# The start of gate/up, the first loads of down, and the stores of the output, reordered in a one-core decoder step

## The reference, cut to what matters

```python
xn = rmsnorm(x, norm1_g)
h = x + concat([gla(xn), shortconv(xn), chunkmlp(xn)]) @ w_out     # w_out 2048 x 2048
hn = rmsnorm(h, norm2_g)
y = h + (silu(hn @ w_gate) * (hn @ w_up)) @ w_down                 # DFF = 5632
out = rmsnorm(y, final_g)
```

## Time and profile before

| what | value |
|---|---|
| median of 3 runs | 2264.31 us (2262.87 to 2264.34) |
| the profiled execution, its own time | 2265.7 us |
| its span, first to last instruction | 2264.0 us |
| PE busy | 2225.8 us (98%) |
| DVE busy | 1599.5 us (71%) |
| ACT busy | 944.4 us (42%) |
| DMA, mean over the span | 144 GB/s |
| mean granted clock of PE | 0.990 |

### The profile page before, as it was taken

The page is one execution under the profiler, slowest core; times in us unless marked ns, Lnnn a source line. Parts: engine busy times, 40 slices in busy tenths (PEclk is TensorE's granted clock), DMA queues, the critical chain, the costliest instruction groups (busy, mean ns, idle before and its releaser), DMA issues.

```text
span 2264.0 us, 41288 instructions
## 1 busy us (share of the span) xinstructions
PE 2225.8 (98%) x17551; PEld 2214.6 (98%) x17551; DVE 1599.5 (71%) x1866; ACT 944.4 (42%) x1235; POOL 10.5 (0%) x16
## 2 busy tenths in 40 slices
PE   9999999999999989999999999999999899999997
PEld 9999999999999989999999999999999899999997
DVE  6346544447444468888888888888888788887787
ACT  6334122114233344444444444444444444444454
POOL 0000000000000000000000000000000000000000
PEclk9999999999999989999999999999999999999998
DMA  5222242453233223544544544544546865555523
GB/s 192 84 75 76 81 159 91 135 180 119 91 103 113 94 95 103 163 137 137 162 137 137 162 137 136 162 137 138 160 137 204 311 225 200 205 188 187 203 87 108
DMA packets 122693, 325.41 MB, mean 144 GB/s; under 512 B 10603, under 2 KB 55211, under 8 KB 121548
## 3 DMA queue, kind: packets, MB, share of 16 engines
q1 hardware_dynamic: 122044, 323.69, 42.5%
q10 hardware_dynamic: 528, 0.07, 0.0%
HBM read 267.09 MB, written 56.63 MB: 143 GB/s over the span
## 4 chain that ended last, share of the span: by engine, by line
PE 89%; DVE 5%; DMA 2%; issue 1%; ACT 1%; SPq 0%; DVEq 0%; ACTq 0%
PE acc L1073 32%; PE acc L867 31%; PE g L1073 23%; DMA w_raw<-w_d 2%; DVE w_lo L1582 1%; DVE w_s L1603 1%; ACT w_hi L762 1%; DVE trunk L1646 1%; DMA h_dram<-hst 0%; PE g L894 0%; DVE w_raw L1603 0%; PE g L1007 0%; PE g L993 0%; DVE trunk L1774 0%; PE g L999 0%
## 5 line engine op out<-in xcount | busy, mean ns | idle before, releaser
L867 PE MATMUL acc<-op_hi,w_hi 128*128 128x272 f32 x1920 | 402.1, 291 | 1.3 <-DVE w_lo L1191 1.3
L867 PE MATMUL acc<-op_hi,w_lo 128*128 128x272 f32 x1920 | 398.7, 289 | 0.0
L867 PE MATMUL acc<-op_lo,w_hi 128*128 128x272 f32 x1920 | 397.0, 288 | 0.0
L762 ACT CAST w_hi<-w_s 128x1024 fp32r<-128x1024 f32 (+1 forms) x204 | 209.6, 1028 | 366.5 <-DVE w_s L1603 366.5
L1073 PE MATMUL g<-op_hi,w_hi 128*128 128x272 f32 x1056 | 308.1, 292 | 10.8 <-ACT g L738 5.5
L1073 PE MATMUL acc<-op_hi,w_hi 128*128 128x272 f32 x1056 | 306.5, 290 | 5.0 <-DVE w_lo L1582 4.2
L867 PEld LDWEIGHTS acc<-op_hi,w_hi 128*128 128x128 f32 x1920 | 303.7, 189 | 4.5 <-issue 3.5
L1073 PE MATMUL g<-op_hi,w_lo 128*128 128x272 f32 x1056 | 307.3, 291 | 0.0
L1073 PE MATMUL acc<-sg_hi,w_hi 128*128 128x272 f32 x1056 | 306.8, 291 | 0.0
L1073 PE MATMUL acc<-sg_hi,w_lo 128*128 128x272 f32 x1056 | 306.6, 290 | 0.0
L1073 PE MATMUL g<-op_lo,w_hi 128*128 128x272 f32 x1056 | 305.8, 290 | 0.0
(11 more groups left out here) (258 smaller groups left out, 4178.1 us busy)
## 6 DMA issues: line engine op xcount, KB each, us to landing
w_raw<-w_in SPq DMA_DIRECT2D x88, 512.0 KB, 3.3
w_raw<-w_gu SPq DMA_DIRECT2D x88, 512.0 KB, 3.6
w<-w_gu SPq DMA_DIRECT2D x88, 512.0 KB, 3.2
hf_dram<-hf_hi SPq DMA_DIRECT2D x22, 952.0 KB, 6.4
hf_dram<-hf_lo SPq DMA_DIRECT2D x22, 952.0 KB, 8.7
w_raw<-w_out SPq DMA_DIRECT2D x32, 512.0 KB, 3.2
w_raw<-w_d SPq DMA_DIRECT2D x32, 512.0 KB, 4.1
w<-w_d SPq DMA_DIRECT2D x32, 512.0 KB, 3.2
```

Of the source, the lines that this page charges most:

```text
L762: nc.scalar.copy(w_hi[:, (C_ST + n) % RING, 0:w], src[:, 0:w]).then_inc(hi_ready, 1)
L867: last = nc.tensor.matmul(acc[t % 2][:, a, 0:TH], w, x[:, k, a * TH:(a + 1) * TH], start=start and n == 0, stop=stop and n == 2)
```

## The change

Three places are edited.

1. **The first difference forms.** Difference forms 0 and 1 (which now hold combinations 0 and 3, through `T_OF`) are built in two parts: pairs 0 to 6 (1904 columns) during the last tile of w_out, once its first chunk has read tiles 0 to 7, and pair 7 (272 columns) at the end. `forms(i - 1)` moves from the third to the second of a tile pair's four steps. Forms 2 and 3 are built whole, with the weights' lo parts 4 and 5 between them on DVE. PE waits for the last pair only ahead of that pair.
2. **Loads of down.** The loads that SP issued behind the four weight blocks of a unit are now issued between them, by `between(s, j)` after each `load_block(s, j)`. The last spill is split over two units.
3. **The end.** Stores go out from two queues: SP stores tiles 0, 4 and 8 (pairs of tiles), ACT tiles 2, 6, 10 and tiles 12 to 15 as one transfer. The column sums of the last squares move behind the first `factor`.

```diff
+T_OF = (0, 3, 1, 2)
...
+            def between(s, j):
+
+                c, b = divmod(s - FT, BATCHES)
+                if c:
+                    if b and c < NCH - 1 and j != 1:
+                        p = 3 * (b - 1) + (3, 0, 2).index(j)
+                        if p < NP:
+                            sp.wait_ge(chunk_done, done(NP * (FT + BATCHES * c) - NP + p))
+                            load_form(c + 1, p)
+                elif b == 1:
+                    if j == 1:
+                        load_h(1)
+                    elif j == 2:
+                        spill_last(0)
+                    else:
+                        load_form(1, (3, 0).index(j))
+                elif b == 2:
+                    if j == 1:
+                        spill_last(1)
+                    elif j == 2:
+                        sp.wait_ge(hf_out, 32 * (FT // 2))
+                        load_h(2)
+                    else:
+                        load_form(1, 2 + (3, 0).index(j))
+                else:
+                    if j == 1:
+                        load_h(3)
+                    else:
+                        load_form(1, 4 + (3, 0, 2).index(j))
...
                 for j in (1, 3, 0, 2):
                     load_block(s, j)
-                c, b = divmod(s - FT, BATCHES)
-                if c == 0 and b == 1:
-                    load_h(1)
-                    spill_hidden(FT // 2 - 1)
...
+                    between(s, j)
...
-                nc.scalar.copy(opf_hi[:, f], xg[:, :, f, :]).then_inc(t_hi, 1)
+                act.wait_ge(t_made, 3 * end)
+                nc.scalar.copy(opf_hi[:, f, at:end], xg[:, at:end, T_OF[f], :]).then_inc(t_hi, 1)
...
+                if c == C_ST - 2:
+                    form_t_hi(0, 0, HK - 1)
+                    form_t_hi(1, 0, HK - 1)
             single_hi(HK - 1)
-            form_t_hi(0, 0)
-            form_t_hi(3, 1)
+            form_t_hi(0, HK - 1, HK)
+            form_t_hi(1, HK - 1, HK)
             block_hi(0, 4)
-            form_t_hi(2, 2)
-            form_t_hi(1, 3)
+            form_t_hi(2, 0, HK)
             block_hi(0, 5)
+            form_t_hi(3, 0, HK)
             block_hi(0, 6)
...
-                if s == 2 and i:
+                if s == 1 and i:
                     forms(i - 1)
+                if c == C_ST - 2:
+                    form_t_lo(0, 0, HK - 1, 1)
             dve.wait_ge(acc_free, N_IN + KT)
             dve.nop().then_inc(c_read, 8)
+            form_t_lo(1, 0, HK - 1, 2)
             forms(HK - 1)
-            for n, f in enumerate((0, 3, 2, 1)):
-                form_t_lo(f, n)
+            form_t_lo(0, HK - 1, HK, 3)
+            form_t_lo(1, HK - 1, HK, 4)
+            block_lo(0, 4)
+            form_t_lo(2, 0, HK, 5)
+            block_lo(0, 5)
+            form_t_lo(3, 0, HK, 6)
             add_square(KT - 1)
-            for idx in (4, 5, 6):
-                block_lo(0, idx)
+            block_lo(0, 6)
...
+            for a in (1, 0):
+                for k in range(2, NV_OUT, 4):
+                    act.wait_ge(out_v, k // 2 + 1 + (1 - a) * NV_OUT // 2)
+                    act.dma_start(yT[:, k:k + 2, a * TH:(a + 1) * TH], trunk[:, k:k + 2, a * TH:(a + 1) * TH])\
+                        .then_inc(stored, 16)
+                act.wait_ge(out_p, 2 * (2 - a))
+                act.dma_start(yT[:, NV_OUT:, a * TH:(a + 1) * TH], trunk[:, NV_OUT:, a * TH:(a + 1) * TH])\
+                    .then_inc(stored, 16)
...
-            column_sums(0, (rstd[:, 0:TH], sq4[3][:, 0, :], sq4[3][:, 1, :]))
+            column_sums(0, (rstd[:, 0:TH],), True, False)
             pe.wait_ge(diagonals, 1)
             factor(1, pb, 0)
+            pe.wait_ge(part_sq, 4)
+            column_sums(0, (sq4[3][:, 0, :], sq4[3][:, 1, :]), False, True)
             factor(1, pb, 1)
```

More of the change, by code:

```diff
@@ L222, in build @@
         sq4 = [b.rearrange("p (q t) -> p q t", q=2) for b in (tmp[:, 0, :], tmp[:, 1, :], gate, up)]
-        form_hi = (sg_hi[:, 0], opf_hi[:, 0], opf_hi[:, 3], sg_hi[:, 1], opf_hi[:, 1], sg_hi[:, 2], opf_hi[:, 2])
-        form_lo = (sg_lo[:, 0], opf_lo[:, 0], opf_lo[:, 3], sg_lo[:, 1], opf_lo[:, 1], sg_lo[:, 2], opf_lo[:, 2])
+        form_hi = (sg_hi[:, 0], opf_hi[:, 0], opf_hi[:, 1], sg_hi[:, 1], opf_hi[:, 2], sg_hi[:, 2], opf_hi[:, 3])
+        form_lo = (sg_lo[:, 0], opf_lo[:, 0], opf_lo[:, 1], sg_lo[:, 1], opf_lo[:, 2], sg_lo[:, 2], opf_lo[:, 3])
         h_dram = nc.dram_tensor("h_dram", (P, KT, T), F32).ap()
@@ L478, in _, with spill_last @@
             load_h(0)
+            def spill_last(i):
+                d, t = ((hf_dram[0], hf_hi), (hf_dram[1], hf_lo))[i]
+                sp.wait_ge(hf_rdy, FT // 2)
+                sp.dma_start(d.rearrange("f p j t -> p f j t")[:, :, FT // 2 - 1, :], t[:].bitcast(F32))\
+                    .then_inc(hf_out, 16)
+            def between(s, j):
[26 more added lines that the diff above has]
+                        load_form(1, 4 + (3, 0, 2).index(j))
             for s in range(FT + 1, NS):
@@ L481, in _ @@
                     load_block(s, j)
-                c, b = divmod(s - FT, BATCHES)
-                if c == 0 and b == 1:
-                    load_h(1)
-                    spill_hidden(FT // 2 - 1)
[L486 to L494, removed]
+                    between(s, j)
             for a in (1, 0):
-                for k in range(0, KT, 2):
-                    made, n = (out_v, k // 2 + 1) if k < NV_OUT else (out_p, (k - NV_OUT) // 2 + 1)
-                    sp.wait_ge(made, n + (1 - a) * (NV_OUT if k < NV_OUT else KT - NV_OUT) // 2)
+                for k in range(0, NV_OUT, 4):
+                    sp.wait_ge(out_v, k // 2 + 1 + (1 - a) * NV_OUT // 2)
                     sp.dma_start(yT[:, k:k + 2, a * TH:(a + 1) * TH], trunk[:, k:k + 2, a * TH:(a + 1) * TH])\
                         .then_inc(stored, 16)
-            sp.wait_ge(stored, 16 * (1 + 1 + KT))
+            sp.wait_ge(stored, 16 * (1 + 1 + NV_OUT + 2))
             sp.wait_ge(cmv_out, 16)
@@ L716, in single_hi, with form_t_hi @@
                 nc.scalar.copy(sg_hi[:, 1:3, i, :], xg[:, i, 2:4, :]).then_inc(sg_h, 1)
-            def form_t_hi(f, n):
-                if n == 0:
+            def form_t_hi(f, at, end):
+                if end < HK:
+                    act.wait_ge(chunk_done, C_ST - 1)
+                else:
                     act.wait_ge(chunk_done, C_ST)
-                    act.wait_ge(t_made, 3 * HK)
-                nc.scalar.copy(opf_hi[:, f], xg[:, :, f, :]).then_inc(t_hi, 1)
+                act.wait_ge(t_made, 3 * end)
+                nc.scalar.copy(opf_hi[:, f, at:end], xg[:, at:end, T_OF[f], :]).then_inc(t_hi, 1)
             def sides(s):
@@ L1101, in quad, with ready @@
                     if first and idx in T_AT:
-                        pe.wait_ge(t_rdy, T_AT.index(idx) + 1)
+                        f = T_AT.index(idx)
+                        pe.wait_ge(t_rdy, f + 1 if f < 2 else f + 3)
+                        if f < 2:
+                            def ready(j, f=f):
+                                if j == HK - 1:
+                                    pe.wait_ge(t_rdy, f + 3)
                     if first and idx == 0:
@@ L1140, in _, with column_sums @@
                     product(C_ST + NP * s + idx, NP * s + idx, (0, 1), PAIRS_H[ch], 4 * (ch % 2))
-            def column_sums(a, bufs):
+            def column_sums(a, bufs, first, last):
                 for n, buf in enumerate(bufs):
-                    if a == 0 and n == 1:
-                        pe.wait_ge(part_sq, 4)
                     for j in range(3):
                         at = BLOCKS[j][0]
-                        last = nc.tensor.matmul(pa[:, a, j:j + 1], buf[:, at:at + P], onesf[:, 0:1],
-                                                start=n == 0 and j == 0, stop=n == len(bufs) - 1, skip_group_check=True)
-                last.then_inc(var_done, 1)
+                        mm = nc.tensor.matmul(pa[:, a, j:j + 1], buf[:, at:at + P], onesf[:, 0:1],
+                                              start=first and n == 0 and j == 0, stop=last and n == len(bufs) - 1,
+                                              skip_group_check=True)
+                if last:
+                    mm.then_inc(var_done, 1)
             def factor(a, bank, side):
@@ L1161, in _ @@
             pe.wait_ge(part_add, 4)
-            column_sums(1, (rstd[:, TH:T],))
-            column_sums(0, (rstd[:, 0:TH], sq4[3][:, 0, :], sq4[3][:, 1, :]))
+            column_sums(1, (rstd[:, TH:T],), True, True)
+            column_sums(0, (rstd[:, 0:TH],), True, False)
             pe.wait_ge(diagonals, 1)
             factor(1, pb, 0)
+            pe.wait_ge(part_sq, 4)
+            column_sums(0, (sq4[3][:, 0, :], sq4[3][:, 1, :]), False, True)
             factor(1, pb, 1)
@@ L1569, in forms, with form_t_lo @@
                 differences(xg[:, i], t_made, 3 * i)
[L1571 to L1574, removed]
+            def form_t_lo(f, at, end, n):
```

(3 more changed lines are left out.)

## The result

The changed kernel takes 2288.73 us (median of 4 runs, 2287.94 to 2289.42) against 2264.32 before: **24.4 us slower, ratio 1.0109 (95% interval 1.0091 to 1.0126)**. The direction was forecast, the size was not: 8.5 us were expected, and the range ended at 2281.

What follows compares the result with a forecast made beforehand. PE, busy 98%, was taken as the bound, with a closed loop through block 0's load in down's three-pair units. Terms -4.2 + 2.7 + 6.9 + 3.1 + 0 = +8.5 us on 2264.3 gave 2272.8 us, range 2258 to 2281.

Steps and rivals of the forecast that it cites:

- The loop from block 0 to block 0: Down, three-pair units: a closed loop of 16.8 us, 4.25 of it block 0's transfer; a later block 0 delays PE equally.
- I take the middle, 2.3: Down, units 49 to 51: a form pair issued ahead of block 0 delays it 2.3 us, between 1.9 and 2.8.
- Units 49 to 51: Down, three-pair units: block 0's delay of 2.3 us counts three times, +6.9 us (5.7 to 8.4).
- Units 53 to 63: Down, four-pair units: 0.7 us lost per unit beyond the room, +3.1 us (0.7 to 7.9).
- The room of 1.6 us: Down, four-pair units: PE's unit takes 21.2 us, DVE's loop is shorter, so 1.6 us of delay per unit is hidden.
- Chunk 0: Start of down, units 45 to 47: later block 0 loads, partly offset by a smaller gap, +2.7 us (+1 to +4).
- Difference forms: Start of gate/up: forms built earlier remove the 3.73 us gap ahead of product 1, -4.2 us (-5.5 to -2.5).
- 2.1 us more idle time ahead of gate/up: Before gate/up: DVE's lo part of form 0 precedes the last residual, so PE starts 2.1 us later, at 819.8.
- The end: Last column sums, scaling and stores: earlier first scaling and two store queues gain nothing, 0 us (-1.2 to +0.9).
- forms don't hold up block 0: Rival for down's loads: DMA serves short transfers beside long ones, added delay near 0, 2253.6 us; chance 0.15.
- the loop has more slack: Rival for down: pairs pack at 1.9 us or less, four-pair units absorb them, about 2266 us; chance 0.13.
- the new gaps pull the clock down: Rival for units 44 to 51: 2 to 4 us gaps at product 6 lower PE's clock, 2279 us; chance 0.10.

Runs made afterwards that it cites:

- chunk0_only: Changed kernel with the form pairs from chunk 1 on issued behind the four blocks again, only chunk 0's transfers between blocks: 2265.05 us, ratio 1.0007 to before.
- tiny_pair: Changed kernel, but from chunk 1 on two 128 x 16 byte transfers between blocks 3 and 0, form pairs behind block 2: 2266.70 us, ratio 1.0013 to before.
- half_pair: Changed kernel, but from chunk 1 on only one form's hi half (544 KB) between blocks 3 and 0, the rest behind block 2: 2275.15 us, ratio 1.0045.
- forms_alone: Kernel before with only the difference forms of the change: 2257.96 us, ratio 0.9982 to before.
- loads_back: Changed kernel with the loads of down issued as before, behind a unit's four blocks: 2259.03 us, ratio 0.9985 to before.
- loads_alone: Kernel before with only the loads of down issued between the blocks: 2290.95 us, ratio 1.0120 to before.

## Why the prediction was wrong

**Right in kind.** The loop from block 0 to block 0 is the bound in three-pair units, and what stands ahead of block 0 in SP's queue lengthens it: `chunk0_only`, `tiny_pair` and `half_pair` show it. Most signs that were named came: no gap ahead of product 1, about 4 us at product 6 of unit 44 (4.18), a smaller one at unit 45, block 0 landing 5.9 us or more after its issue behind a pair, PE idle in units 53 to 63. Two were off: the idle time ahead of gate/up is 6.83 us, not 8, and units 49 to 51 were to last about 19 us, where the loops that end at their block 0 take 19.7, 20.2 and 20.7.

**The step that failed** is the size of the delay that a pair adds: "I take the middle, 2.3", with 1.9 if all is packed and 2.8 if block 0 keeps its lag behind block 3. It measured 3.0, 3.5 and 4.2 us in units 49 to 51. The landings of unit 49 show where it went wrong. The lo half lands 1.4 us behind the hi half and block 0 1.0 behind that, which is packed at 400 GB/s. But the hi half lands 2.6 us behind block 3, 1.2 more than its bytes take. Before, block 0 stood in that place and landed 1.9 us behind block 3, 1.0 more than its bytes take. This lag stayed, and the pair's 2.8 us came on top: the upper bound was the right one, and averaging it with 1.9 was the mistake. What adds another 0.5 and 1.2 us in units 50 and 51 stays open; `tiny_pair`, with no bytes to speak of, shows part of it (0.4 and 1.0). The one number enters three times:

- *Units 49 to 51:* 3 x 2.3 = 6.9 forecast, 10.7 measured; 3.0 + 3.5 + 4.2.
- *Units 53 to 63:* forecast 3.1, measured 15.0. This term is a small difference, delay less room. The room of 1.6 us that the rows gave was right: where PE does not hold the loop up, it takes 14.2 us from the use of block 0 to the issue of the next block 3 (1905.22 to 1919.42 in the changed kernel), which leaves 7.0 of PE's 21.2, and before the change block 0 landed 5.4 us after the issue of block 3 in the mean of the nine units that have a pair. Now it lands 8.8 us after it, 3.4 later (2.3 to 4.7). With 3.4 in place of 2.3 the recorded sum gives 13.0 of the 15.0. By the starts of the units the changed kernel loses 1.7, 3.5 and 1.3 us in chunk 2, 1.8, 1.9 and 1.3 in chunk 3 and 1.3, 1.1 and 1.0 in chunk 4. PE itself never catches up in a chunk's first unit (units 56 and 57 both start 14.4 us late, units 60 and 61 both 19.5), but the loop gets back most of the 1.6 us that I had counted on: from block 0 of unit 59 to that of unit 60 it takes 19.8 us, not 21.2 (2065.11 to 2084.90). That the room is real, `half_pair` shows as well.
- *Chunk 0:* forecast 2.7, measured 6.4. Set back by the 9.2 us by which unit 44 starts earlier, block 0 of unit 45 is used at 1778.3, where I had 1777.7. Block 1 of unit 46 lands 1.0 us later than I had it. In units 46 and 47 block 0 lands 8.1 and 8.2 us behind block 1, where my packed sums had about 6.8: 1.4 more in each. These three make up the miss of 3.7 us. The gap at unit 45 is 3.21, not 2.3.

The sum with the measured numbers is -5.7 + 6.4 + 10.7 + 15.0 = 26.4. Less the 3.5 us of the mixers that is 22.9, and with 0.3 behind the last unit the 23.2 us between the spans (2264.0 and 2287.2).

**Difference forms.** -4.2 forecast. The trace of the changed kernel has -5.7, just outside the bound of -5.5; `forms_alone` has -5.1 by the medians and `chunk0_only`, which has the same edit there, -4.5 in its trace. The gap of 3.73 us went as forecast. The forecast of 2.1 us more idle time ahead of gate/up was right as well, only the changed kernel's own profile hides it. In the trace of `chunk0_only` the first matmul and ACT's first hi part of gate/up are

```profile
818.11 0.60 PE L1147 MATMUL g<-sg_hi,w_hi 128*128 128x272 f32 x1 [8.07 <-DVEq L1752]
```

```profile
798.64 1.05 ACT L787 CAST w_hi<-w_raw 128x1024 fp32r<-128x1024 f32 x1 [9.55 <-DMA w_raw<-w_gu]
```

and in the changed kernel the hi part is

```profile
795.55 1.05 ACT L788 CAST w_hi<-w_raw 128x1024 fp32r<-128x1024 f32 x1 [8.29 <-DMA w_raw<-w_gu]
```

The idle time is 8.07 us in the first, and 5.97 + 2.1 is 8.07. The hi part, from which the chain to the last residual goes on, began 11.40 us ahead of the end of w_out in `chunk0_only` (810.04), 11.46 in the kernel before (800.25 against 811.71), and 12.66 in the changed kernel. In each kernel with the edit the lead and the idle time make up the same sum: 11.40 + 8.07, 11.57 + 7.91 in `loads_back`, 12.14 + 7.34 in `forms_alone`, 12.66 + 6.83 in the changed kernel, each 19.47 to 19.49; before it is 17.43, which is 2.05 less. So in the changed kernel's trace some 1.2 of the 1.5 us beyond the forecast come from block 0 of gate/up landing earlier. Why it did, no run settles.

**The end.** 0 forecast, 0.5 (-1.4 to +3.2) measured. That two queues bring no bandwidth agrees with the trace after: the DMA engines move 3.48 MB in the 10 us from 2275 at 348 GB/s, against 346 before.

**The rivals.** That forms don't hold up block 0 is refuted by `loads_alone`; that the loop has more slack, by the 10.7 us of units 48 to 51. The third, that the new gaps pull the clock down, came true as to the clock, but not as to the time: PE alone after the gap at unit 44 of the changed kernel,

```profile
1771.00:1778.00 7.00, 6.47 (x30) 0.53 0.40 142
```

is at the lower level. In units 49 to 51 the mean granted clock is below 1 as well (0.93 from 1850 to 1870 us), and still the loop without its transfers takes the 11.6 us of before, so there the clock costs nothing. The loss in units 53 to 63 happens at a granted clock of 1.00 (191.1 us of PE work in the 200 from 1950), so it is not the clock's. In chunk 0 what the lower clock costs beside the waits no run separates.

What is left open is what makes the delay grow from unit 49 to unit 51 (in unit 51 the lo half lands 2.5 us behind the hi half, not 1.4), and why the units of chunk 2 lose more (6.5 us) than those of chunk 4 (3.4). Most of that is one unit: block 0 of unit 55 lands 10.3 us after the issue of block 3, the lo half ahead of it 4.2 us behind the hi half, where it was 1.4 in unit 49.

## What to carry to other kernels

The transfers of SP's queue landed in the order of issue here, so a bulk transfer belongs behind the loads that a closed loop waits for, not between them: look for the load whose landing an engine waits for in each round, count the bytes ahead of it, and ask for it first. Then look for the load that is next in line; here block 2 took over where block 0 was on time and a pair stood behind it. When a row shows a lag and another reading leaves it out, don't average the two: find out whether the lag stays. Where a cost is a small difference between a delay and the room for it, work out the sum at both ends of the delay: 1.1 us more here made 3 us into 15.

## What the runs showed of the hardware that was not expected

- Two transfers of 2 KB each, issued right behind a block, held SP for 1.74 us in unit 49 of `tiny_pair`, and the block after them was used at the same time all the same (5.2 us after block 3's issue against 5.1). The length of the issue row was time that otherwise lay inside the next transfer's latency: 3.0 us where it was 4.2. Two units later the same transfers did cost 1.0 us.
- The same mixer code ran 3 us slower in one profile (granted clock 0.89 over 30 us) than in another (1.00 over 27 us), with PE busy throughout.
- In units 49 and 50 of the changed kernel the first 0.557 MB behind block 3 landed 2.6 and 2.8 us after it, the next 0.557 MB 1.4 us after the first, and block 0's 0.393 MB 1.0 us after those: about 1.2 us of lag behind block 3, none between the others. In units 51 and 55 the second 0.557 MB took 2.5 and 4.2 us; why, no run settles.
